# Output stage of a hybrid decoder step: router input from the normalised rows, nine tiles in the first routing group, the sample tile reordered

## The reference, cut to what matters

```
mix  = concat(y_pool, y_lru) @ w_out
x    = LayerNorm(ALPHA * x + (1 + g1) * mix, ln1_g, ln1_b)
u2   = x * (1 + sc2) + sh2
g_logits = u2 @ w_group + b_group          # 4 groups
e_logits = u2 @ w_route + b_route          # 16 experts, 4 to a group
top group, then the 2 best experts of it   # argmax, top_k
y    = the two experts' gated MLP of u2, weighed
x    = LayerNorm(ALPHA * x + (1 + g2) * y, ln2_g, ln2_b)
```

## Time and profile before

| | us |
|---|---|
| median of 3 runs | 1268.67 |
| lowest and highest | 1266.45, 1276.56 |
| the profiled execution's own time | 1275.0 |
| its span in the trace, first to last instruction | 1271.9 |

### The profile page before, as it was taken

The page is one execution under the profiler, slowest core; times in us unless marked ns, Lnnn a source line. Parts: engine busy times, 40 slices in busy tenths (PEclk is TensorE's granted clock), DMA queues, the critical chain, the costliest instruction groups (busy, mean ns, idle before and its releaser), DMA issues.

```text
span 1271.9 us, 23068 instructions
## 1 busy us (share of the span) xinstructions
PE 1145.7 (90%) x6565; PEld 927.3 (73%) x6566; DVE 895.7 (70%) x1881; ACT 541.6 (43%) x941; POOL 513.1 (40%) x535
## 2 busy tenths in 40 slices
PE   4898999999997988999994289999999999999757
PEld 0597998898895976878772268888888888888511
DVE  2787988898896896566587885666676666643367
ACT  0445444544533532223221344555665555533334
POOL 1502202211220217666651124544655544554368
PEclk9799999999997998999997589999999999999955
DMA  9623203303314354444441757788997796565396
GB/s 336 241 68 109 94 40 132 132 13 119 132 51 175 117 182 139 159 157 166 169 152 69 245 169 205 233 229 237 265 273 226 228 292 199 141 133 113 58 335 237
DMA packets 106345, 215.24 MB, mean 169 GB/s; under 512 B 18107, under 2 KB 67775, under 8 KB 103203
## 3 DMA queue, kind: packets, MB, share of 16 engines
q1 hardware_dynamic: 85148, 163.14, 36.6%
q0 software_dynamic: 20736, 50.89, 17.2%
q10 hardware_dynamic: 415, 0.63, 0.2%
HBM read 153.93 MB, written 85.96 MB: 189 GB/s over the span
## 4 chain that ended last, share of the span: by engine, by line
PE 69%; DVE 12%; POOL 4%; DMA 4%; ACT 4%; issue 4%; SPq 1%; POOLq 0%; DVEq 0%; ACTq 0%
PE bank L1745 20%; PE bank L1746 19%; PE bank L1747 19%; PE bank L1696 6%; POOL arena L702 3%; DMA ada_arena<-in_w_ada 2%; PE bank L1766 1%; DVE parts L1124 1%; DVE arena L1165 1%; PE bank L1725 1%; DMA z_d<-arena,dst_now 1%; DMA arena<-in_w_ada 1%; ACT arena L796 1%; ACT L775 1%; PE bank L1773 1%
## 5 line engine op out<-in xcount | busy, mean ns | idle before, releaser
L1745 PE MATMUL bank<-parts 128*128 128x256 f32 (+2 forms) x1616 | 571.9, 354 | 13.2 <-DVE parts L1180 3.6
L1746 PE MATMUL bank<-parts 128*128 128x256 f32 (+2 forms) x1616 | 553.5, 342 | 0.0
L1747 PE MATMUL bank<-parts 128*128 128x256 f32 (+2 forms) x1616 | 553.4, 342 | 0.0
L1745 PEld LDWEIGHTS bank<-parts 128*128 128x128 f32 x1616 | 309.3, 191 | 65.6 <-issue 21.7
L1747 PEld LDWEIGHTS bank<-parts 128*128 128x128 f32 x1616 | 309.1, 191 | 35.8
L1746 PEld LDWEIGHTS bank<-parts 128*128 128x128 f32 x1616 | 309.5, 192 | 31.0
L600 POOL TENSOR_TENSOR arena<-arena 128x256 f32<-128x256 f32 (+1 forms) x36 | 25.9, 721 | 306.0 <-DVE h_last L1236 284.8
L1696 PE MATMUL bank<-ident,arena 128*128 128x128 f32 (+3 forms) x792 | 117.6, 280 | 31.6 <-DVE arena L1330 12.8
L1696 PEld LDWEIGHTS bank<-ident,arena 128*128 128x128 f32 (+3 forms) x792 | 94.7, 146 | 60.7 <-DVE arena L1330 13.9
L982 ACT ACTIVATE arena<-bank,w_now 128x512 f32<-128x512 f32 x96 | 65.9, 687 | 109.3 <-DVE arena L1592 60.4
L1557 DVE TENSOR_TENSOR parts<-arena,parts x90 | 104.7, 1219 | 9.9 <-ACT parts L957 9.9
(11 more groups left out here) (292 smaller groups left out, 1541.4 us busy)
## 6 DMA issues: line engine op xcount, KB each, us to landing
arena<-in_w_ada SPq DMA_DIRECT2D x16, 1024.0 KB, 5.9
arena<-in_w_gate SPq DMA_DIRECT2D x16, 1024.0 KB, 5.5
arena<-in_w_up SPq DMA_DIRECT2D x16, 1024.0 KB, 13.4
arena<-in_w_down SPq DMA_DIRECT2D x16, 1024.0 KB, 15.3
ada_arena<-in_w_ada SPq DMA_DIRECT2D x8, 1024.0 KB, 17.5
arena<-in_x_prompt SPq DMA_DIRECT2D x8, 1024.0 KB, 7.2
yT_d<-arena SPq DMA_DIRECT2D x16, 512.0 KB, 4.3
arena<-yT_d SPq DMA_DIRECT2D x16, 512.0 KB, 4.6
```

Source lines behind the costliest of these rows:

```text
L1745: pe.matmul(out, x_hi, w_hi, start=start, stop=False)
L1746: pe.matmul(out, x_hi, w_lo, start=False, stop=False)
L1747: return pe.matmul(out, x_lo, w_hi, start=False, stop=stop)
```

## The change

- VectorE joins two rows once (`join_rows`): scale' = ln1_g * (1 + sc2) and shift' = ln1_b * (1 + sc2) + sh2, in place of the rows 1 + sc2 and sh2. `ln_out` makes u2 = z * scale' + shift' and so waits for z and not for x1. The sample's rows are joined in the same way in turn 10 of VectorE's loop, with `row_tmp` as scratch.
- `ln_in(t)` waits in addition for x1 of tile t-2, which GpSimd still reads from z. At the start `join_rows` and `ln_out(0)` come ahead of `ln_in(1)`.
- GpSimd makes the low half of tile 3 before x1 of tile 0, and waits for u2 of tile 0 before x1 of tile 0, and for u2 of tile 15 before x1 of tile 15.
- `ROUTE` is tiles 0 to 8 and 9 to 16. The first group's work is spread over four turns of VectorE: 11 (`choose_group`), 12 (`choose_experts`), 13 (the counts, now `count_up`) and 14 (`place_rows`). TensorE's ranks of that group move from `out_proj(16)` to `out_proj(15)`.
- At the end of the stage `place_rows` of the first group is gone from the place between tiles 15 and 16, `ln_out(15)` stands before `router_out(13)`, and `ln_out(16)` before x1 of tile 16.
- SyncE issues the 24 transfers of the sample's rows after `store_tile(4)`, inside its loop of tiles. It stores tile 16 before it loads expert 0.
- ScalarE makes its two parts of the 0/1 matrices ahead of the first three high parts of expert 0.

```diff
--- before.py
+++ after.py
@@ -28,7 +28,7 @@
 W_IN = KD * WIDE
 PARTS = 2 * W_IN + 2 * KD * C
 OUT_EARLY = 6
-ROUTE = ((0, 11), (11, 17))
+ROUTE = ((0, 9), (9, 17))
 GROUP = max(hi - lo for lo, hi in ROUTE)
 FIRST_HI = 3
 ARENA = 21168
@@ -182,6 +182,7 @@
         x1 = [at(13960 + n * 1024, D) for n in range(2)]
         u2 = [at(16008 + n * 1024, D) for n in range(2)]
         row_tiles_s = at(18056, 3, D)
+        row_tmp = at(10816, D)
 
         w_hi, w_lo = part_at(0, 2, WE), part_at(2 * WE, 2, WE)
         xT_hi, xT_lo = part_at(4 * WE, KD, P), part_at(4 * WE + KD * P, KD, P)
@@ -498,18 +499,19 @@
 
             sp.wait_ge(S["y_stored"], 16 * TPC * NCH + 16)
             store_tile(0, 0)
-            with sp.Fori(1, NT // 2 - 1) as j:
-                for b in range(2):
-                    load_next(2 * j + b, b)
-                    store_tile(2 * j + b - 1, 1 - b)
+            for lo, hi in ((1, 3), (3, NT // 2 - 1)):
+                with sp.Fori(lo, hi) as j:
+                    for b in range(2):
+                        load_next(2 * j + b, b)
+                        store_tile(2 * j + b - 1, 1 - b)
+                if lo == 1:
+                    load_sample_rows()
             load_next(NT - 3, 0, NS)
-            load_sample_rows()
             store_tile(NT - 4, 1)
             store_tile(NT - 3, 0)
             store_tile(NT - 2, 1)
-            sp.wait_ge(S["x1_ready"], NT)
+            store_tile(NT - 1, 0, NS)
             load_expert(0, 0, static=True)
-            store_tile(NT - 1, 0, NS)
             sp.wait_ge(S["rt_ok"], NT)
             load_expert(1, 1, static=True)
             sp.dma_start(g2_row, all_parts(mod_d[0, G2:G2 + D])).then_inc(S["g2_in"], 16)
@@ -632,8 +634,9 @@
                 o.step(pool.tensor_tensor(x1[b][0:n, :], z[b][0:n, :], row_tiles[0:n, 1, :], ALU.mult))
                 pool.tensor_tensor(x1[b][0:n, :], x1[b][0:n, :], row_tiles[0:n, 2, :], ALU.add).then_inc(S["x1_ready"], 1)
 
+            y_lo(3, 1)
+            pool.wait_ge(S["u2_ready"], 1)
             x1_tile(0, 0)
-            y_lo(3, 1)
             x1_tile(1, 1)
             with pool.Fori(1, NT // 2 - 1) as j:
                 o.enter(j, 1, 2)
@@ -643,6 +646,7 @@
             o.leave(NT // 2 - 2)
             y_lo(NT - 1, 0, NS)
             x1_tile(NT - 3, 0, NT // 2 - 1)
+            pool.wait_ge(S["u2_ready"], NT - 1)
             x1_tile(NT - 2, 1, NT // 2 - 1)
 
 
@@ -930,12 +934,12 @@
                 cols = slice(n * SPLIT, (n + 1) * SPLIT)
                 act.activation(w_hi[:, 0, cols], w_raw[0][:, cols], ACT.Copy).then_inc(S["w_hi"], 1)
 
+            for k in range(2):
+                act.wait_ge(S["hot_one"], k + 1)
+                act.activation(hot_b[:, k, :, 1, :], hot_b[:, k, :, 2, :], ACT.Copy, scale=part_i[:, 0:1]).then_inc(S["hot_part"], 1)
             act.wait_ge(S["w_raw0"], 48)
             for n in range(FIRST_HI):
                 first_hi(n)
-            for k in range(2):
-                act.wait_ge(S["hot_one"], k + 1)
-                act.activation(hot_b[:, k, :, 1, :], hot_b[:, k, :, 2, :], ACT.Copy, scale=part_i[:, 0:1]).then_inc(S["hot_part"], 1)
 
             act.wait_ge(S["w_exp"], 1)
             act.activation(g_gap, g_gap, ACT.Exp).then_inc(S["w_expd"], 1)
@@ -1299,6 +1303,8 @@
             def ln_in(t, b, n, rows, uses):
 
                 dve.wait_ge(S["mix_ready"], t + 1)
+                if t >= 2:
+                    dve.wait_ge(S["x1_ready"], t - 1)
                 for h in range(2):
                     o.did(dve.tensor_tensor(z[b][0:n, 512 * h:512 * h + 512], bank[2 * b + h][0:n, :],
                                             rows[0][0:n, 512 * h:512 * h + 512], ALU.mult))
@@ -1321,13 +1327,19 @@
                 dve.scalar_tensor_tensor(rs[b][0:n, 1:2], mv[b][0:n, 0:1], -1.0, rs[b][0:n, 0:1], ALU.mult, ALU.mult).then_inc(ready, 1)
 
             def ln_out(t, b, n, rows, uses, first):
-                dve.wait_ge(S["x1_ready"], t + 1)
+                dve.wait_ge(S["z_norm"], t + 1)
                 if not first:
 
                     dve.wait_ge(S[f"u2_st{b}"], 16 * (uses - 1))
                     dve.wait_ge(S["u2T_mm"], 2 * t - 2)
-                o.step(dve.tensor_tensor(u2[b][0:n, :], x1[b][0:n, :], rows[1][0:n, :], ALU.mult))
+                o.step(dve.tensor_tensor(u2[b][0:n, :], z[b][0:n, :], rows[1][0:n, :], ALU.mult))
                 dve.tensor_tensor(u2[b][0:n, :], u2[b][0:n, :], rows[2][0:n, :], ALU.add).then_inc(S["u2_ready"], 1)
+
+            def join_rows(n, scale, shift, tmp):
+
+                o.step(dve.tensor_tensor(tmp[0:n, :], row_tiles[0:n, 2, :], scale[0:n, :], ALU.mult))
+                o.did(dve.tensor_tensor(shift[0:n, :], tmp[0:n, :], shift[0:n, :], ALU.add))
+                o.step(dve.tensor_tensor(scale[0:n, :], row_tiles[0:n, 1, :], scale[0:n, :], ALU.mult))
 
             def router_out(t, n=P):
                 dve.wait_ge(S["rt_mm"], t + 1)
@@ -1376,6 +1388,9 @@
                     o.did(dve.tensor_tensor(g4(e12[:, k, lo:hi]), over_e, hot.unsqueeze(2).to_broadcast([P, n, NGR, EPG]), ALU.mult))
                 o.wait()
                 o.step(dve.tensor_tensor(m_all[:, lo:hi], e12[:, 0, lo:hi], e12[:, 1, lo:hi], ALU.add))
+
+            def count_up(lo, hi):
+
                 for t in range(lo, hi):
                     o.step(dve.tensor_tensor(cum_all[:, t + 1], cum_all[:, t], m_all[:, t], ALU.add))
                 dve.memset(spare[0:1, 0:1], 0.0).then_inc(S["m_ready"], 1)
@@ -1403,10 +1418,11 @@
             o.did(dve.tensor_scalar(off_t, valid[:], -8192.0, 8192.0, ALU.mult, ALU.add))
 
             ln_in(0, 0, P, prompt_rows, 1)
+            dve.wait_ge(S["tiles_in"], 64)
             dve.wait_ge(S["ylru_ready"], NG * NCH + NG)
+            join_rows(P, prompt_rows[1], prompt_rows[2], u2[1])
+            ln_out(0, 0, P, prompt_rows, 1, True)
             ln_in(1, 1, P, prompt_rows, 1)
-            dve.wait_ge(S["tiles_in"], 64)
-            ln_out(0, 0, P, prompt_rows, 1, True)
             ln_in(2, 0, P, prompt_rows, 2)
             ln_out(1, 1, P, prompt_rows, 1, True)
             dve.wait_ge(S["rt_in"], 64)
@@ -1419,23 +1435,27 @@
                         choose_group(lo, hi)
                     if t == hi + 3:
                         choose_experts(lo, hi)
+                    if t == hi + 4:
+                        count_up(lo, hi)
+                    if t == hi + 1:
+                        dve.wait_ge(S["tiles_s_in"], 16 * 3 * DEC_B)
+                        join_rows(NS, sample_rows[1], sample_rows[2], row_tmp)
                     if t == hi + 5:
                         place_rows(lo, hi)
+            ln_out(NT - 2, 1, P, prompt_rows, NT // 2, False)
             router_out(NT - 4)
-            ln_out(NT - 2, 1, P, prompt_rows, NT // 2, False)
-            place_rows(*ROUTE[-2])
-            dve.wait_ge(S["tiles_s_in"], 16 * 3 * DEC_B)
             ln_in(NT - 1, 0, NS, sample_rows, NT // 2 + 1)
             router_out(NT - 3)
-            dve.wait_ge(S["z_norm"], NT)
+            ln_out(NT - 1, 0, NS, sample_rows, NT // 2 + 1, False)
+            router_out(NT - 2)
+            dve.wait_ge(S["x1_ready"], NT - 1)
             dve.wait_ge(S["x1_st0"], 16 * (NT // 2))
             o.step(dve.tensor_tensor(x1[0][0:NS, :], z[0][0:NS, :], row_tiles[0:NS, 1, :], ALU.mult))
             dve.tensor_tensor(x1[0][0:NS, :], x1[0][0:NS, :], row_tiles[0:NS, 2, :], ALU.add).then_inc(S["x1_ready"], 1)
-            ln_out(NT - 1, 0, NS, sample_rows, NT // 2 + 1, False)
-            router_out(NT - 2)
             router_out(NT - 1, NS)
             choose_group(*ROUTE[-1])
             choose_experts(*ROUTE[-1])
+            count_up(*ROUTE[-1])
 
             n_e, slots_n, start_e, end_e = e16[0], e16[1], e16[2], e16[3]
             dve.wait_ge(S["rank_mm"], len(ROUTE))
@@ -1959,7 +1979,7 @@
 
                 router(t - 3, first=t == 3)
                 for lo, hi in ROUTE:
-                    if t == hi + 5:
+                    if t == hi + 6:
                         ranks(lo, hi)
 
             out_proj(2, 0, turn_before=lambda: turn_u2(0, 0, first=True))
```

## The result

The changed kernel takes 1278.83 us (median of 20 runs, 1276.35 to 1283.55), the kernel before beside it 1269.01 (20 runs): ratio 1.0066, 95% interval 1.0049 to 1.0082. Forecast were 1265.6 and a range up to 1273: outside the range, and slower where faster was forecast.

The account below looks back on a forecast made before the run. TensorE was taken to bound the loop, VectorE the tail until the first gather. -3.1 + 1.2 + 4.4 + 1.5 + 2.8 - 11.2 + 1.3 = -3.1 against the median 1268.67 gave 1265.6 us, range 1256 to 1273.

Parts of the forecast that it names:

- Start: Stage start: the 4.58 wait goes, TensorE waits 3.85 at a later sum; -3.1, with +1.2 for the clock.
- That 1.2: Start: half of the 2.5 us lost if TensorE's clock falls after its wait at the sum.
- Burst: SyncE's 24 transfers delay tile 8's yT load: TensorE waits 4.4 once, +1.5 for the clock.
- VectorE's turns 10 to 14: Loop turns with joins and routing portions: net one more late sum and a few tenths, +2.8; bounds 0 and 5.
- The slack of 3.1: In the loop: the lateness of a VectorE turn, 3.1 us, that is absorbed before TensorE's sum is late.
- Tail: Last product to last logits: u2 of tile 15 needs only z, so tile 16 begins 9.9 sooner; -11.2.
- Last portion: Last routing group has eight tiles for six: more counts and 0/1 matrices; +1.3.
- Expert weights: First expert load, issued later, stays hidden by the routing chain before the first gather; cost 0, otherwise 1 to 3.
- Rival 1: The burst hides and the clock holds: the 5.9 goes, 1259.7, down to 1255.7 with more; chance 0.25.
- Rival 2: Slower, by the burst at the yT loads of tiles 8 and 9: 13.4 instead of 5.9, 1273; chance 0.17.

Follow-up runs that it names:

- e1: Kernel before with only the 24 sample-row transfers moved behind the store of tile 4: 1278.03 us, ratio to before 1.0074.
- e4: Changed kernel with x1 of tiles 10 to 14 computed for only 16 of 1024 columns: 1268.55 us, ratio to before 0.9995.
- e10: Kernel before with place_rows of the first group put behind the last router_out but one, GpSimd idle: 1266.54 us, ratio to before 0.9964.
- e9: Kernel before with place_rows of the first group put ahead of the last prompt tile's router input: 1267.67 us, ratio to before 0.9982.
- e5: Changed kernel with the 24 transfers given out in fours behind the stores of tiles 1 to 6: 1276.61 us, ratio to before 1.0036.
- e3: Changed kernel with the sample's rows joined in turn 8 of VectorE instead of turn 10: 1278.63 us, ratio to before 1.0068.

## Why the prediction was wrong

Each term against the execution that it was made for; the parts add up to +3.5 (-2.8 + 6.5 + 9.8 - 11.4 + 1.4), the profiled time rose by 4.2; the other 0.7 are not accounted for.

- **Start, -1.9: measured -2.8** at the second router (512.56 against 502.48 + 12.85). The chain was right: tile 1 is late next, through the low half that holds the scale operation for 2.19. TensorE waited 2.69 for 3.85, and the clock took 1.89 for 1.2. That 1.2 was half of a price, on the reading that the clock had held after a gap of 4.15; it fell just behind that stretch (last section). The greater fault was the choice of execution: a usual run of before has no wait of 4.6 to save. Counted from the products L1940, its second router comes at 32.6 (510.10 - 477.54) and that of the changed kernel at 35.8 (512.56 - 476.74), so against the usual run this part is a loss of 3.3. I read that the profile lay 6.3 above the median and set the sum against the median all the same. With +3.3 in place of -2.8 the parts add up to 9.6; the medians differ by 9.8, and from the usual group of before (1267.8) it is 11.0.
- **Burst, +5.9: measured 6.5**, place, chain and size right for this kernel; in the kernel before the same burst costs 9 (e1). The Trainium skill, "DMA: Bandwidth & Descriptors" (Issuing engines are not separate DMA queues), calls the sequencer's time for starting a transfer usually small relative to the transfer. What counted here is their sum: 24 took 9.00, and TensorE waited for the load behind them.
- **VectorE's turns 10 to 14, +2.8: measured +9.8**, the 13.6 of the last product less the two parts above. **This step failed.** The single prices held: joins 7.9 (8.2 put), two portions 13.7 (13.8), counts 6.1 (6.3), placing 7.75 (9.2). Two things failed.
  - The slack of 3.1 can be used once. After TensorE has waited, VectorE is still that late, and all that a later turn takes too long is paid. By the prediction's own numbers the five turns are 2.8 + 3.0 + 0.9 + 3.8 = 10.5 too long (the 3.0 for turns 11 and 12 together), so 7.4 are paid, less 2.3 of before: 5.1 and not 2.8.
  - The residual sum, which I took to be free of holds, is held as late turns meet GpSimd's low halves: in turns 11 to 14 it took 1.93, 3.37, 3.23 and 1.92 for 1.22, +5.6. The scale operation of turn 10 took 1.69 for 0.16, +1.5.
  - Together: 10.5 less the 2.05 that the prices were too high, and 7.1 more, is 15.6. From one product L1309 to the next the five turns (603.76 to 683.18) took 15.2 more than five periods. VectorE is still 3.3 late at the end, 11.9 are TensorE's four periods. Before was 0.3 over, and the last projection gave 1.9 back (before's wait of 1.28, and the rank products that moved): 9.8.
  - It is paid elsewhere than predicted. The waits of 1.41, 2.48 and 3.83 stand at the sums of projections 12 to 14, behind the join and the two portions. Counts and placing brought none: behind the 3.83 TensorE lost 3.0 more at the lower clock (0.50 in 660.0 to 666.0), and in that time VectorE's lateness fell to 0.9. e4 shows the holds from the other side.
- **Tail, -11.2: measured -11.4.**
- **Last portion, +1.3: measured +1.4**, from the last logits to the first expert product 32.67 (738.31 - 705.64), before 31.31.
- **Expert weights, 0: as put.** The gather came 24.4 behind the last logits and waited for no weights.

Rival 1 is refuted by the burst's 6.5. Rival 2 had the kernel slower, but by the wrong mechanism: its price lay in the burst, not in VectorE. The tail's gain was real and was paid ahead of it: work taken from an idle tail was put where VectorE had 3 us left and GpSimd held its port.

## What to carry to other kernels

Before work is moved into a loop, sum the moved engine's time over all the turns concerned, with the slack counted once, and ask for each turn which instructions of the other engine on its port will run then; a small operation costs what it is held, not what it does. Move work into idle time in which the port partner is idle too (e10), not into idle time spent waiting for the partner (e9). And check which of a kernel's groups of times the profile at hand belongs to before a sum is set against a median.

## What the runs showed of the hardware

- One-column and integer operations are held as well: L1327 on 128x1 took 2.19 for 0.16, L1394 on int32 (e9) 2.21 for 0.18. Not held beside a GpSimd instruction: reductions (L1359 at 628.52, 0.18) and products with one input in PSUM (L1309 at 620.54, 1.28) in the changed kernel, the statistics (L1313 at 615.44, 1.29 the pair) and their one-column `tensor_scalar` (L1318 at 617.01, 0.15) in the kernel before. The Trainium skill, "SBUF — State Buffer" (Who interferes with whom), says that reductions never contend, that an instruction with two SBUF inputs does and `tensor_scalar` can, and that the blocked side waits for the whole instruction; the rows agree. Of the two integer `tensor_scalar` steps of placing one was held (L1409, 2.26) and one, which began with GpSimd's sum, was not (L1408, 0.18).
- The granted clock after waits of TensorE, in the changed kernel's view by stretches:

```profile
499.00:502.00 3.00, 0.44 (x2) 0.01 (x1) 2.97 (x3) 1.33 (x2) 1.61 (x1) 1.00 0.00 0
502.00:503.50 1.50, 1.38 (x5) 1.19 (x6) 1.11 (x2) 0.07 (x1) 1.43 (x1) 0.61 0.00 0
503.50:506.00 2.50, 2.50 (x12) 2.26 (x11) 0.00 (x0) 0.82 (x2) 2.42 (x2) 0.55 0.77 298
```

 Full through the wait of 2.69, near the lower level (1.2 GHz) behind it; in the wait of 3.83 it fell within the wait, and stood at 0.50 from 659.5 on. With a fall a period was longer than its wait by 1.89 (start), 1.87 (burst) and 3.02 (660), without one by 0.3 (waits of 1.41 and 2.48). The earlier trace rows seem to show a gap of 4.15 without a fall, but they end at 685.00; the next stretch of the kernel before, with the transposes (from 684.24) still running, is

```profile
685.00:686.00 1.00, 0.64 (x6) 0.53 (x3) 0.86 (x6) 1.00 (x2) 0.00 (x0) 0.57 0.93 369
```

 The length of a wait alone does not tell. Behind 2.48 in the changed kernel and behind 2.49 in e5, at the sums of projections 13 and 12:

```profile
643.50:646.50 3.00, 3.00 (x19) 2.49 (x20) 2.96 (x3) 1.09 (x2) 3.00 (x1) 1.00 0.40 162
...
626.50:629.50 3.00, 3.00 (x11) 2.60 (x12) 2.96 (x3) 0.10 (x1) 3.00 (x1) 0.50 0.35 141
```

 In e3 a wait of 2.01 made its period 1.88 longer still. What decides stays open.
- The same program starts this stage in two ways, 5.9 us apart at the first router product, by which engine takes the port first: GpSimd first by 0.09 to 0.38 us in five traces, VectorE first by 0.17 to 0.18 in three.
